# Three modulation pieces multiplied side by side: the adaLN projection of a two-layer diffusion block

## What the reference computes

```python
mod_lat = (jax.nn.silu(c) @ w_ada[l] + b_ada[l])[:, None, :]      # (1, 1024) @ (1024, 6144)
mod_ctx = jax.nn.silu(c_ctx) @ w_ada[l] + b_ada[l]                # the same weights
sh1, sc1, g1, sh2, sc2, g2 = jnp.split(mod_lat, 6, axis=-1)
h_lat = modulate(rms_norm(x, norm_mix[l]), sh1, sc1)              # feeds everything that follows
```

## Time and profile before

| | us |
|---|---|
| median of 3 runs | 2723.68 |
| lowest, highest | 2714.36, 2724.6 |
| span of the profiled execution | 2709.9 |
| L625 multiplies, both layers, busy | 174.5 |
| L625 idle before, waiting for data | 25.2 |

### The profile page before, as it was taken

The page is one execution under the profiler, slowest core; times in us unless marked ns, Lnnn a source line. Parts: engine busy times, 40 slices in busy tenths (PEclk is TensorE's granted clock), DMA queues, the critical chain, the costliest instruction groups (busy, mean ns, idle before and its releaser), DMA issues. The chain is left out here.

```text
span 2709.9 us, 30557 instructions
## 1 busy us (share of the span) xinstructions
PE 2348.9 (87%) x9676; PEld 1365.1 (50%) x9677; DVE 1105.0 (41%) x2043; ACT 620.8 (23%) x1256; POOL 383.3 (14%) x372
## 2 busy tenths in 40 slices
PE   6899869999999948999887799599999997599990
PEld 1255446777775534444421455367777654344440
DVE  0045555444541143333334355644454312433335
ACT  0133334333331110111100243333333211011110
POOL 0033300000003311001011243100000032010002
PEclk9899989999999978999999899799999998699995
DMA  9401005000012216657789111020000121578845
GB/s 346 160 25 52 26 16 206 9 8 9 9 41 100 93 69 225 234 186 279 286 332 391 46 41 33 20 74 9 8 9 7 70 92 71 200 252 277 294 169 186
DMA packets 164581, 336.04 MB, mean 124 GB/s; under 512 B 10726, under 2 KB 91644, under 8 KB 163756
## 3 DMA queue, kind: packets, MB, share of 16 engines
q1 hardware_dynamic: 121388, 215.67, 22.5%
q10 hardware_dynamic: 30464, 73.50, 7.0%
q0 software_dynamic: 12672, 46.14, 4.8%
HBM read 271.65 MB, written 72.02 MB: 127 GB/s over the span
## 5 line engine op out<-in xcount | busy, mean ns | idle before, releaser
L880 PE MATMUL PS<-KV,R 128*128 x832 | 381.5, 613 | 30.3 <-DMA KV<-in_w_down 9.2
L745 PE MATMUL PS<-KV,R 96*128 96x512 f32 (+1 forms) x800 | 327.6, 518 | 4.8 <-ACT ZO L1061 3.6
L771 PEld LDWEIGHTS PS<-KV,R 128*128 128x128 f32 x2624 | 315.5, 192 | 11.0 <-issue 3.3
L771 PE MATMUL PS<-KV,R 128*128 128x64 f32 x2624 | 309.1, 272 | 2.6 <-ACT R L1058 1.3
L880 PEld LDWEIGHTS PS<-KV,R 128*128 128x128 f32 x832 | 160.6, 196 | 245.1 <-issue 245.1
L802 PE MATMUL PS<-KV,R 128*128 128x512 f32 x576 | 257.6, 601 | 2.7 <-ACT R L1078 2.7
L1461 DVE COPY R<-PS 128x256 f32<-128x256 f32 (+1 forms) x272 | 149.6, 550 | 248.8 <-PE PS L751 248.8
L1449 DVE TENSOR_REDUCE sm<-PS 128x1 f32<-128x1280 f32 (+1 forms) x144 | 197.7, 1373 | 123.1 <-PE PS L745 123.1
L751 PE MATMUL PS<-CST,R 128*128 128x128 f32 x1312 | 217.1, 279 | 15.7 <-ACT R L1050 1.9
L751 PEld LDWEIGHTS PS<-CST,R 128*128 128x128 f32 x1312 | 154.8, 147 | 113.3 <-ACT ZO L1061 43.0
L625 PE MATMUL PS<-KV,SC 128*2 128x512 f32 x384 | 174.5, 613 | 29.3 <-DMA KV<-in_w_ada 25.2
(11 more groups left out here) (232 smaller groups left out, 2445.8 us busy)
## 6 DMA issues: line engine op xcount, KB each, us to landing
KV<-in_w_ada ACTq DMA_DIRECT2D x22, 2048.0 KB, 19.2
KV<-in_w_gate SPq DMA_DIRECT2D x32, 1024.0 KB, 9.2
KV<-in_w_up SPq DMA_DIRECT2D x32, 1024.0 KB, 11.3
KV<-in_w_down SPq DMA_DIRECT2D x32, 1024.0 KB, 13.4
yb_d<-R ACTq DMA_DIRECT2D x52, 512.0 KB, 6.8
xmid_d<-R SPq DMA_DIRECT2D x18, 512.0 KB, 2.6
f_d<-R SPq DMA_DIRECT2D x18, 512.0 KB, 2.8
R<-xnext_d SPq DMA_DIRECT2D x18, 512.0 KB, 4.0
```

Source lines behind the costliest of these rows:

```text
L745: mm = pe.matmul(bank(b + i, 0, w), QS[0:QK, h, :], kT[0:QK, h, 512 * i:512 * i + w], start=True, stop=True)
L771: mm = pe.matmul(bank(7, 0, VDIM), pT[h % 2][:, j, :], V[:, j * 512 + h * VDIM:j * 512 + (h + 1) * VDIM], start=(j == 0), stop=(j == nk - 1))
L880: mm = pe.matmul(bank(2 + u), bT[u][:, kk, :], KV[:, bass.ds(off + kk * 512, 512)], start=(kk == 0), stop=(kk == KD - 1))
```

## The change

The three pieces of a turn are multiplied after all three have landed, in one loop with the contraction step outside and the piece inside. Piece u writes PSUM partitions 32u and 32u+1 of bank u, which places its two stationary columns in the column strip 32u of the array. The three signals `ada_mm` come with the last contraction step. ACT's copies read and write the same partitions; the three result rows then share their columns of SBUF. Counts, sizes and order of DMAs are unchanged.

```diff
-        arow = [R2[0:2, 4096 + 512 * u:4608 + 512 * u] for u in range(3)]
+        arow = [R2[32 * u:32 * u + 2, 4096:4608] for u in range(3)]
@@ tensor engine
                 def ada(j, l=l):
                     for u in range(3):
                         pe.wait_ge(ada_in[u], 16 * (j + (ADP // 3 * l + 1)))
-                        ge(pe, arow_ready, 3 * j + (ADP * l + u - 2))
-                        for kk in range(KD):
-                            mm = pe.matmul(PS[0:2, u, :], SC[:, kk, :], wada[u][:, kk, :], start=(kk == 0), stop=(kk == KD - 1))
-                        mm.then_inc(ada_mm, 1)
+                    ge(pe, arow_ready, 3 * j + ADP * l)
+                    for kk in range(KD):
+                        for u in range(3):
+                            mm = pe.matmul(PS[32 * u:32 * u + 2, u, :], SC[:, kk, :], wada[u][:, kk, :],
+                                           start=(kk == 0), stop=(kk == KD - 1))
+                            if kk == KD - 1:
+                                mm.then_inc(ada_mm, 1)
@@ scalar engine
-                        act.activation(arow[u], PS[0:2, u, :], ACT.Copy).then_inc(arow_ready, 1)
+                        act.activation(arow[u], PS[32 * u:32 * u + 2, u, :], ACT.Copy).then_inc(arow_ready, 1)
```

## The result

The changed kernel takes 2773.23 us (median of 4 runs, 2768.85 to 2781.64), the kernel before 2719.02 (4 runs, 2713.44 to 2724.6). The ratio is 1.0208, with a 95% interval of 1.0181 to 1.0236: slower, clear of noise, though whether by more than 2% is open. The forecast was slower, 2803 us, and its range 2762 to 2880 holds the time. But the likeliest case isn't what happened; the one called "full overlap of three strips" is, and it had said 2775 us. The range reached from that case to no overlap at all, so that it holds the time says little.

What follows compares the result with a forecast made beforehand. Layer 0's modulation was taken as bound by PE, by a small margin, layer 1's by transfers. +38.3 and +41.3 gave +79.6 on a span of 2709.9, 2789.5; with 13.8 for the median, 2803 us, range 2762 to 2880.

Steps and rivals of the forecast that it cites:

- the likeliest case: Both modulations: the strips overlap only pairwise, a turn takes 12.9 us, total 2803 us; chance 0.38.
- full overlap of three strips: Rival for both modulations: three strips run fully in parallel, a turn takes 9.0 us, +51, total 2775 us; chance 0.28.
- no overlap at all: Rival for both modulations: the strips don't overlap, a turn takes 22.8 us, +147, total 2871 us; chance 0.27.
- T and R add: Modulation: multiplying a turn (T) and landing its three successors (R), overlapped before, now follow one another; 12.9 and 18.3 us.
- R, 18.3 us: Modulation: time from a turn's end to the landing of its three successors, alone on the queue: 0.36 + 7.7 + 10.2.
- T, 12.9 us: Modulation: PE's time for a turn of three pieces, with pairwise overlap of strips and 2.0 us for the clock.
- The clock, 2.0 us a turn: PE's slower start after idling about 18 us before each turn adds 2.0 us, from a span of 1.5 to 2.4.
- Start of the first turn, 42.0: Layer 0: the first three pieces have landed and their turn begins at 42.0 us (41.4 to 43.1).
- ACT's tail, +1.75 us: End of modulation: ACT finds three results at once where it found one; two more copies and stores add 1.75 us.
- Layer 1: Its modulation, sharing DMA with the combining of expert outputs: +41.3 us in the main forecast, +27 + 1.15 under full overlap.
- The step from span to median, 13.8 us: Whole kernel: the runs' median exceeds the span of 2709.9 by 13.8 us, added to the forecast span of 2789.5.
- Not slower: Rival: three loads in flight move faster than one; R = 7.4 us leaves layer 0 even, total 2701 us; chance 0.03.

Runs made afterwards that it cites:

- Experiment 4: The kernel before, waiting for one piece at a time, each piece multiplied as two halves of 256 columns in two strips: 2701.81 us, 0.9944 of before.
- experiments 2: The changed kernel with the loops exchanged, all 16 multiplies of one strip before those of the next: 2790.14 us.
- 6: The changed kernel with runs of two products (four multiplies) on a strip before the next strip: 2772.73 us.
- 8: The changed kernel with runs of four products (eight multiplies) on a strip before the next strip: 2797.39 us.
- experiment 3: The changed kernel with 20 unused products ahead of each turn's waits, to keep the clock up: 2762.79 us, 1.0169 of before.
- Experiment 7: The changed kernel with the change in layer 0 alone, layer 1's modulation as before: 2745.8 us, 1.0113 of before.
- experiment 9: The kernel of Experiment 4, with layer 0's mixer weights loaded only after its last modulation piece has landed: 2692.18 us, 0.9926 of before.
- experiment 1: The changed kernel with all three pieces in one strip (array columns 0 and 1), wait and order of multiplies kept: 2853.46 us.
- quarters: As Experiment 4, but each piece in four strips of 128 columns, with four copies and four stores: 2698.66 us, 0.9924 of before.

## Why the prediction was right, and where it was wrong

**T and R add.** Right, and it decides the sign. Each gap ends with a landing, and next to no transfer runs in layer 0's turns. Experiment 4 keeps the strips, takes the wait for three away, and turns +54 us into -15.

**R, 18.3 us.** Measured 18.29, 18.54 and 18.41 us. One landing of 7.7 us plus two transfers of 5.1 at 410 GB/s was the right reading of the earlier trace rows: the three loads behind the first turn, issued at 50.67, 52.28 and 54.72, took 7.8, 11.3 and 14.0 us to land, so they landed 5.1 us apart.

**T, 12.9 us. This step failed.** It put the two halves of a product in each other's way ("if multiplies leave in program order and a strip takes one at a time"). They did leave in order, as far as the times tell, but a strip takes some four at a time (experiments 2, 6, 8). With runs of two multiplies no strip ever blocks, and three run at once: 9.0 us. The rows that I took for it show that a product is two instructions; they say nothing on how many a strip can hold, and I should have given that no weight. 3.9 us on 8 turns are 31 us, about as much as the whole miss of 30 between 2803 and 2773. Two smaller errors, below, nearly cancel.

**The clock, 2.0 us a turn.** Measured 1.9 in layer 0 (experiment 3: 7.04 against 8.9 to 9.0), 1.5 to 2.0 in layer 1.

**Start of the first turn, 42.0.** Measured 41.64.

**ACT's tail, +1.75 us.** In the changed kernel TensorE ends at 132.67 and the first tile begins at 135.55, 2.88 us; before it was 0.94 (111.94 to 112.88). So +1.9. Layer 0 by the full-overlap rival: +22.7, measured +22.7.

**Layer 1.** The rival's walk, 27 + 1.15, gave +28; measured 29.5. Its parts were less good than its sum. I gave the combining 274 GB/s during a turn, and it took 151 in the first turn, though 266 in the second:
```profile
1425.00:1433.50 8.50, 8.47 (x48) 1.43 (x42) 6.50 (x6) 0.00 (x0) 3.36 (x7) 0.82 0.45 151
1471.80:1480.80 9.00, 8.99 (x48) 1.57 (x48) 6.48 (x7) 0.00 (x0) 3.02 (x4) 0.78 0.75 266
1436.00:1470.00 34.00, 0.00 (x0) 0.00 (x0) 18.19 (x17) 0.73 (x2) 10.91 (x16) 0.53 1.03 413
```
Beside the load behind the first turn the combining moved 9.25 MB (q0 and q1, 1433.5 to 1471.8 us) and not 6.0, so that load took 38.30 us and not 32.7. The next one took 29.25 and not 32.7, as only 5.0 MB were left to share with. The two errors nearly cancel in the sum.

**What no step held.** 3.8 us between the modulations and 1.1 behind: full overlap gives 51, the span shows 57.1. Experiment 7 finds such a remainder too, in the tiles behind layer 0's modulation. Most of the first part is the clock in the tiles behind layer 0's modulation. TensorE's second group of L647 there, before and after (L650):
```profile
147.71 5.86 PE L647 MATMUL PS<-KV,R 128*128 128x416 f32 x16 [2.31 <-DVE R L1377]
```
```profile
171.73 7.55 PE L650 MATMUL PS<-KV,R 128*128 128x416 f32 x16 [2.31 <-DVE R L1380]
```
The group ahead of it took 7.35 us before and 8.64 after. In the stretches from one tile to the next that hold the two groups the granted clock was 0.84 and 1.00 before, 0.78 and 0.91 after. That is 3.0 us, and the shift of the tiles grows by as much (22.7 to 25.7). With halves the two groups took 8.39 and 7.50 us, in experiment 9 7.33 and 5.85. So the slower pair also comes without the wait for three, and the faster one also with strips; what sets it was not found.

**The step from span to median, 13.8 us, and some luck.** It came from one span and three runs that lie 10 us apart. With a fourth run the median before is 9.1 us above that span (2719.02 against 2709.9), and after the change it is 6.2 above (2773.23 against 2767.0). The medians differ by 54.2 us. The miss of 30 us is thus 22.5 in the span (79.6 forecast, 57.1 measured) and 7.6 in this term. It also means that the 2775 us of full overlap came so close by luck: its shift was 6.4 us too small, and this term 7.6 too large.

**A wrong sum in the last rival.** "Not slower" sets 42.0 + 36 + 3R + 1.75 = 111.94 and reads R = 7.4 us. It gives R = 10.7, so 6.29 MB would have to come at some 590 GB/s, not 850. The measured gaps (18.3 us at 407 GB/s) rule it out all the same.

**The rule on weight loads and row groups.** The Trainium skill, page "TensorE: Matmul & The Clock Gate", section "The mechanism", says that weight loads overlap running multiplies only when the row groups differ, and by that the loads here would have waited. The same section also excepts loads that target a background weight buffer; no run here shows which buffer a load used. This case's trace does not agree with the rule without that exception: with three strips of one row group the loads leave three at a time every 0.43 us, and the multiplies lose nothing. The 2.38 times of its section "Measured speedup vs the span model" is below what is seen here: warm, three pieces in 7.04 us against the 20.75 of three warm pieces in a row, 2.95 times; with the clock's slow start in both, 8.9 to 9.0 us against 22.4 to 23.7 in experiment 1, some 2.5 times.

## What to carry to other kernels

Making the engine that looks like the bound three times faster can lose, if the grouping that it takes stops the transfers that ran behind it. Add work and transfer for the new grouping before counting the speed-up: here 9.0 + 18.4 against 20.6 us. Take the parallelism inside the unit that a buffer holds, so that buffers still come free one at a time, and stop when transfers are the bound (halves were enough, quarters gave no more).

## What the runs showed of the hardware

Three multiplies of 128 x 2 by 128 x 512 in float32, in three column strips, ran at the rate of one, 0.43 us. How far apart in program order multiplies for different strips may stand is limited: alternation after 2 or 4 gave full overlap, after 8 the turn was 14 to 15 us, after 16 it was 19 to 20. In the kernels with full overlap a turn behind a gap of 13 us or more took 1.3 to 2.9 us longer than the 7.04 us behind a gap of 1 us, and behind 2.63 us it took 1.7 us longer (experiment 3). And the read of the 96 rows took 6.5 us from issue to use behind 5.2 MB of weights (85.36 to 91.89 in experiment 9); in experiment 4, where little else moved, it took 1.65 in layer 0 (95.41 to 97.06) and 1.8 in layer 1 (1479.41 to 1481.20).
